# Moving the decayed keys of a chunked gated recurrence ahead of the last level's scores

## The reference

```python
b = jnp.cumsum(lc, axis=1)                      # cumulated log decay inside a chunk
diff = b[:, :, None] - b[:, None, :]
dec = jnp.where(causal, jnp.exp(jnp.minimum(diff, 0.0)), 0.0)
scores = jnp.einsum('bthk,bshk,btshk->btsh', qc, kc, dec)
intra = jnp.einsum('btsh,bshv->bthv', scores, vc)
inter = jnp.einsum('bthk,bhkv->bthv', qc * jnp.exp(b), s)
b_last = b[:, -1]
kd = kc * jnp.exp(b_last[:, None] - b)          # decayed keys
s_new = s * jnp.exp(b_last)[..., None] + jnp.einsum('bshk,bshv->bhkv', kd, vc)
```

## Time and profile before

| | |
|---|---|
| median of 3 runs | 1444.94 us |
| profiled execution, its own time | 1447.3 us |
| its span, first to last instruction | 1445.6 us |
| mean granted TensorE clock | 0.909 |
| TensorE matmul busy | 1197.0 us (83%) |
| VectorE busy | 513.9 us (36%) |
| ScalarE busy | 197.6 us (14%) |
| HBM traffic over the span | 283 GB/s |

### The profile page before, as it was taken

The page is one execution under the profiler, slowest core; times in us unless marked ns, Lnnn a source line. Parts: engine busy times, 40 slices in busy tenths (PEclk is TensorE's granted clock), DMA queues, the critical chain, the costliest instruction groups (busy, mean ns, idle before and its releaser), DMA issues.

```text
span 1445.6 us, 14774 instructions
## 1 busy us (share of the span) xinstructions
PE 1197.0 (83%) x5922; PEld 648.0 (45%) x5922; DVE 513.9 (36%) x991; ACT 197.6 (14%) x320; POOL 261.2 (18%) x568
## 2 busy tenths in 40 slices
PE   4799899998998969889989967888778888877840
PEld 2345555654555646556657643333233333333310
DVE  2402466465354464236552263211111122111107
ACT  1301010100211221042220140000000000000003
POOL 4070088884000000011120000000000000001010
PEclk9899999999998879889999987999988999999985
DMA  9999567865666447441232345999999999999944
GB/s 340 373 346 341 186 221 240 283 207 199 235 232 219 147 171 262 160 133 59 73 107 69 120 171 183 419 421 414 420 411 401 397 404 410 408 402 402 402 172 145
DMA packets 140086, 387.02 MB, mean 268 GB/s; under 512 B 15211, under 2 KB 54501, under 8 KB 112558
## 3 DMA queue, kind: packets, MB, share of 16 engines
q1 hardware_dynamic: 132208, 361.91, 66.6%
q0 software_dynamic: 6528, 18.72, 3.8%
q10 hardware_dynamic: 1280, 5.42, 1.1%
HBM read 385.95 MB, written 23.13 MB: 283 GB/s over the span
## 4 chain that ended last, share of the span: by engine, by line
PE 45%; DMA 27%; POOL 10%; DVE 10%; issue 3%; SPq 3%; ACT 2%; POOLq 0%; DVEq 0%; ACTq 0%
DMA slot<-in_w_exp_up 20%; PE psum L1462 10%; PE psum L1100 10%; PE psum L1387 5%; PE psum L1133 4%; DMA slot<-in_w_ada 3%; PE psum L1029 3%; PE psum L999 3%; POOL mem L557 2%; POOL sq L558 2%; POOL sq L555 2%; POOL mem L560 2%; DMA mem<-in_w_exp_down 2%; POOL sq L559 2%; POOL sq L556 2%
## 5 line engine op out<-in xcount | busy, mean ns | idle before, releaser
L1462 PE MATMUL psum<-slot,mem 128*64 128x512 f32 x1024 | 253.3, 653 | 70.5 <-DMA slot<-in_w_exp_up 69.7
L1100 PE MATMUL psum<-hT,slot 128*128 128x320 f32 (+1 forms) x1056 | 304.9, 449 | 0.0
L1100 PEld LDWEIGHTS psum<-hT,slot 128*128 128x128 f32 (+1 forms) x1056 | 203.0, 195 | 98.7 <-issue 25.4
L1462 PEld LDWEIGHTS psum<-slot,mem 128*64 128x64 f32 x1024 | 81.1, 150 | 234.0 <-issue 156.4
L2206 DVE TENSOR_TENSOR sq<-sq,psum 128x256 f32<-128x256 f32 x16 | 6.7, 421 | 329.2 <-ACT sq L934 329.2
L1486 PE MATMUL psum<-mem,sq 128*64 128x512 f32 x512 | 113.4, 595 | 9.4 <-issue 6.1
L999 PE MATMUL psum<-slot,cT 128*8 128x512 f32 (+1 forms) x768 | 103.4, 647 | 19.0 <-DMA slot<-in_w_ada 19.0
L627 POOL DMA_INDIRECT moe_output<-mem,idx x16 | 16.2, 1011 | 484.3 <-ACT mem L938 484.3
L1387 PE MATMUL psum<-mem,slot 128*128 128x320 f32 x256 | 70.8, 440 | 5.4 <-DVE mem L2021 5.4
L1133 PE MATMUL psum<-mem,slot 128*128 128x320 f32 x256 | 74.6, 448 | 0.0
L1486 PEld LDWEIGHTS psum<-mem,sq 128*64 128x64 f32 x512 | 41.0, 137 | 71.5 <-issue 68.0
(11 more groups left out here) (449 smaller groups left out, 1287.6 us busy)
## 6 DMA issues: line engine op xcount, KB each, us to landing
slot<-in_w_ada SPq DMA_DIRECT2D x48, 2048.0 KB, 9.5
slot<-in_w_exp_gate SPq DMA_DIRECT2D x64, 1024.0 KB, 13.9
slot<-in_w_exp_up SPq DMA_DIRECT2D x64, 1024.0 KB, 16.3
mem<-in_w_exp_down SPq DMA_DIRECT2D x32, 2048.0 KB, 17.7
slot<-in_w_in SPq DMA_DIRECT2D x17, 2048.0 KB, 10.6
slot<-in_w_out SPq DMA_DIRECT2D x8, 2048.0 KB, 8.1
mem<-in_w_in SPq DMA_DIRECT2D x2, 2048.0 KB, 18.1
mem<-in_x_prompt ACTq DMA_DIRECT2D x1, 2048.0 KB, 12.3
```

Source lines behind the costliest of these rows:

```text
L1100: last = mm(psum[0:wd, grp % 2, 0:T], w[:, k, q * P:q * P + wd], hT[:, k, :], start=(k == 0), stop=(k == KD - 1))
L1462: last = mm(psum[rows_, 0, :].rearrange("p (w n) -> p w n", w=2), xe[i % 2][:, k, rows_], gate_up[h][:, :, k, :], start=(k == 0), stop=(k ...
```

## The change

`hg_kd` is put in another order, and exp(hb) gets a buffer and a place of its own. The new buffer `hX` is the last 640 columns of the work area, used by nothing else while the recurrence runs. At level 2, behind that level's own exponential, ScalarE writes exp(hb) into `hX`. In `hg_kd` VectorE starts with b_last - b into `hE`, copies the chunk decays out of `hX`, multiplies the keys, and only then takes the scores of level 6 and makes the decayed queries. The memset that served as a signal is gone. TensorE's `hg_out` waits for the decayed queries as well, since they now come later.

```diff
+        hX = ar(7168, 640)
@@ ScalarE
                 if lv:
                     act.wait_ge(S("hg_expo"), 6 * hp + lv)
                     st(s.activation(hE, hE, ACT.Exp), "hg_exp")
+                if lv == 2:
+                    if hp:
+                        act.wait_ge(S("hg_qk"), 7 * hp)
+                    st(s.activation(hX, hb, ACT.Exp), "hg_exp2")
 
             def hg_kd(hp):
-                act.wait_ge(S("hg_expo2"), 2 * hp + 1)
-                st(s.activation(hE, hb, ACT.Exp), "hg_exp2")
-                act.wait_ge(S("hg_expo2"), 2 * hp + 2)
+                act.wait_ge(S("hg_expo2"), hp + 1)
                 st(s.activation(hE, hE, ACT.Exp), "hg_exp2")
@@ TensorE, hg_level and hg_out
-                    pe.wait_ge(S("hg_qk"), 6 * hp + lv)
+                    pe.wait_ge(S("hg_qk"), 7 * hp + lv)
...
                 pe.wait_ge(S("hg_sc_used"), 7 * (hp + 1))
+                pe.wait_ge(S("hg_qk"), 7 * (hp + 1))
@@ VectorE
             def hg_kd(hp):
                 q_, k_ = (flat[:, (x + 2 * hp) * T:(x + 2 * hp + 2) * T] for x in (HQ, HF))
-                hg_take(hp, 6)
-                st(v.memset(small[:, 60:61], 0.0), "hg_expo2")
+                e3, b3, x3 = (t.rearrange("p (n r) -> p n r", r=CH) for t in (hE, hb, hX))
+                st(tt(e3, bc(b3[:, :, CH - 1:CH], [P, 10, CH]), b3, SUB), "hg_expo2")
                 dve.wait_ge(S("hg_exp2"), 2 * hp + 1)
-                st(tt(hq_, q_, hE, MUL))
-                e3, b3 = (t.rearrange("p (n r) -> p n r", r=CH) for t in (hE, hb))
-                st(v.tensor_copy(small[:, 80:90].unsqueeze(2), e3[:, :, CH - 1:CH]))
-                st(tt(e3, bc(b3[:, :, CH - 1:CH], [P, 10, CH]), b3, SUB), "hg_expo2")
+                st(v.tensor_copy(small[:, 80:90].unsqueeze(2), x3[:, :, CH - 1:CH]))
                 dve.wait_ge(S("hg_exp2"), 2 * hp + 2)
                 st(tt(hE, k_, hE, MUL), "hg_kd")
+                hg_take(hp, 6)
+                st(tt(hq_, q_, hX, MUL), "hg_qk")
```

## The result

| | before | changed |
|---|---|---|
| median of 5 runs | 1444.94 us (1443.33 to 1447.03) | 1431.84 us (1428.75 to 1434.70) |
| ratio, 95% interval | | 0.9909 (0.9891 to 0.9926) |
| profiled execution, span | 1445.6 us | 1430.1 us |
| mean granted TensorE clock | 0.909 | 0.911 |

A forecast was written before the change was run, and what follows sets the result against it. TensorE, almost gapless in the scans, was held by waits for decayed keys and a lowered clock behind them. Removing 4.13 + 4.14 us idle and 2.63 + 2.57 us clock loss took 1444.94 to 1431.5 us, range 1426.5 to 1437.5.

The forecast's parts named there:

- Removed wait: TensorE's idle time before turning the decayed keys goes entirely: 4.13 us in the first pass, 4.14 in the second.
- rival B: Keys come slightly late, leaving 0.6 to 0.8 us idle per pass without a clock fall: 1432.9 us, chance 0.06.
- Clock: Key turning and its bulk piece take 9.42 us at full clock, saving 2.63 and 2.57 us; bounded 0 to 5.20.
- Rivals A and D: A: wait goes, clock stays low, 1436.7 us, chance 0.13; D: clock low for the whole bulk piece, 1450.3 us, chance 0.04.
- The second fall: Clock drop behind the state products L1229, slowing the next bulk piece; expected to stay, 3.3 us either way.
- The exponential at level 2: Moved exp(hb), 0.74 us on ScalarE twice, hidden by idle time before evacuation L742: cost 0, uncovered 1.5 us.
- The moved take and product: VectorE's level 6 take and query product after the keys: cost 0 with 6.1 us cover; uncovered, 1.94 us per pass.
- What follows: Gain passes on in full through the second pass's long wait and the expert stream, whose first loads wait for TensorE's L1387.
- Rival C: No change: the expert stage gives the gain back, its weight stream ending when it did before; 1444.9 us, chance 0.04.
- The sum: Idle time and clock savings over both passes: 4.13 + 4.14 + 2.63 + 2.57 = 13.47 us.

The follow-up runs named there:

- filled gap: Kernel before, with seven unread 128x320 matmuls on TensorE ahead of its wait for the decayed keys, both passes: 1439.32 us, ratio 0.9962.
- gap put back: Changed kernel with seven scratch products on VectorE ahead of the product with the keys, both passes: 1449.15 us over 12 runs, ratio 1.0013.
- take first: Changed kernel with the level 6 take again ahead of the subtraction, exp(hb) keeping its buffer and place at level 2: 1438.25 us, ratio 0.9938.
- exponential in the key step: Changed kernel with exp(hb) moved from level 2 to behind the exponential of the keys, own buffer kept: 1431.86 us, ratio 0.9909.
- exponential fourfold: Changed kernel with the exponential of hb at level 2 done four times instead of once, both passes: 1433.29 us, ratio 0.9907.
- matmuls added: Changed kernel with seven unread 128x320 matmuls on TensorE ahead of its wait for the decayed keys: 1437.78 us, ratio 0.9951 to the kernel before.

## Why the prediction was right

- *Removed wait.* 4.13 and 4.14 us were forecast. The distances up to the turnings fell by 76.99 - 72.78 = 4.21 and 121.20 - 116.81 = 4.39. The margin of 0.22 us in the first pass came out at 0.26: product done at 446.74, 0.06 to TensorE, turning started at 447.06. In the second it was 0.47 where 0.42 was worked out: product done at 572.76, turning started at 573.29. With no gap left, rival B falls. It was ScalarE's queue that decided, as said.
- *Clock.* 2.63 and 2.57 were forecast, 12.05 - 9.42 = 2.63 and 11.99 - 9.43 = 2.56 came. The filled gap and the gap put back show that the term hangs on the gap. Rivals A and D fall with it. The statement of the Trainium skill on transposes (TensorE: Matmul & The Clock Gate, section "Part 4: PE-mode transpose") is not borne out here: float32 transposes with a thin modulation piece ahead kept a clock of 1.00 in the changed kernel, and the distance of 9.4 us in every profile with less than 0.2 us of gap ahead. Six transposes in 0.87 us are a weak test of it; a run of 32 that raised the clock is shown in the last section.
- *The second fall* stayed where it was in these two profiles: the bulk piece took 10.37 and 10.31 us in the two passes before, 10.43 and 10.47 now. That it would stay was left open with 3.3 us either way, and this is luck in part: in six other profiles one pass had it at 8.81 us.
- *The exponential at level 2* cost nothing, and neither did three more. *The moved take and product* were done 6.2 us ahead of need; 6.1 was worked out.
- *What follows.* The stretch from the conv states to the end is 808.53 and 808.59 us: all of it starts earlier and ends earlier by the same amount. Two executions alone would not show this to 0.1 us, since the stretch varies by 6 us. But over all profiles it starts between 608.96 and 637.07 us, 28 us apart, and always takes 806.9 to 813.2. Rival C falls.
- *The sum* was 13.47 us; the same places in the profiles give 13.79, the medians 13.10. That 1431.84 came within 0.4 us of 1431.5 is closer than runs of 1428.75 to 1434.70 can bear out; the distances at each place are the better evidence.

One thing in the working was not shown by the rows of before: that the long wait of the second pass would keep its length, because its chain starts from L1252 (L1256 now). It went from 13.48 to 13.06 us. What is fixed is the distance from L1256 to level 1. It is 41.38 or 41.39 us in the changed kernel and in the five kernels built from it that leave the chain alone (take first, exponential in the key step, exponential fourfold, matmuls added, gap put back), while the wait within it ranges from 12.05 to 13.10 us with TensorE's own pace. In the old order it is 41.74, filled or not; I don't know where the 0.36 us come from. So the gain of the first pass did reach the wait unshortened.

For the clock I had bounded the term from 0 to 5.20 us. The distance of the same form at full clock in the earlier trace rows was the right row to go by: it was met to 0.01 us in both passes of the changed kernel.

## What to carry to other kernels

When an engine waits for a chain that crosses two others, look at what the chain's last product really needs. Here it needed neither the last scores nor exp(hb), and the order of the code had put both ahead of it; a buffer for 640 columns was the price of taking them out. Add to a gap of TensorE what the clock costs behind it: here a gap of 4.1 us cost 6.8. And an engine's work that is merely in the way, as the step size function was, can be found by asking of each instruction in the waited-for chain who reads its result.

## What the runs showed of the hardware that I had not expected

- Gaps shorter than the 4.1 us of before brought the clock down too: 2.87 us in one kernel, and 2.05 us in one pass out of two of another. In the same profiles a gap of 1.48 us, ahead of level 1 of the first pass, did not.
- The length of the gap alone doesn't decide. Ahead of the turning of the conv states all thirteen profiles have a gap of 2.14 or 2.15 us, between the same instructions; the clock behind it was 1.00 in seven of them and 0.50 in six. And behind the state products, with 0.77 us of idle time in the midst of thin matmuls, it fell in most passes (the bulk piece took 9.87 to 11.60 us) and in six of the 26 it did not (8.81 us).
- Transposes can raise the clock. In the changed kernel, behind an idle time of 5.10 us, TensorE does 32 float32 transposes (L1421) from 844.09 us and nothing else until 850.11. Windows of 1 us, columns as above:

```profile
848.00:849.00 1.00, 1.00 (x6) 0.85 (x5) 0.00 (x0) 0.74 (x2) 0.00 (x0) 0.50 0.00 0
849.00:850.00 1.00, 1.00 (x10) 0.94 (x8) 0.00 (x0) 0.78 (x3) 0.00 (x0) 0.88 0.00 0
```

- Matmuls that nobody reads, put in the place of a wait, made the kernel before 5.6 us faster (ratio 0.9962, 0.9948 to 0.9975).
- Executions differ by several us in a stretch that is the same code in all these kernels: from the conv states to the end of the span it took 806.9 to 813.2 us over the profiles. Some 3 us can come from the fall behind the 2.14 us gap: from the conv states to the next transposes (L1285) it took 5.79 us in the changed kernel, where the clock stayed at 1.00, and 8.70 in the one with both exponentials in the key step, where it was 0.50.
